# Last norm of a two-layer decoder trunk: tile 0 finished on ScalarE and GpSimd, tile 1 on VectorE, one Newton step for both

## The reference, cut to what matters

```
def layer_norm(x, g, b):
    xf = x.astype(jnp.float32)
    mu = xf.mean(-1, keepdims=True)
    var = jnp.square(xf - mu).mean(-1, keepdims=True)
    y = (xf - mu) * lax.rsqrt(var + LN_EPS) * g.astype(jnp.float32) + b.astype(jnp.float32)
    return y.astype(x.dtype)

# per layer l: mixer, first norm, then
y = hier_moe(u, w_grp[l], b_grp[l], w_router[l], b_router[l], w_gate[l], w_up[l], w_down[l])
x = layer_norm(ALPHA * x + (1 + gt2) * y, ln2_g[l], ln2_b[l])
```

## Time and profile before

| what | value |
|---|---|
| median of three runs | 802.78 us |
| the profiled execution, its own time | 802.34 us |
| span of its trace | 800.6 us |
| VectorE busy over the span | 394.2 us (49%) |
| ScalarE busy | 99.2 us (12%) |
| GpSimd busy | 72.7 us (9%) |
| mean DMA rate over the span | 365 GB/s |

### The profile page before, as it was taken

One profiled execution on the slowest core, in us unless ns is written; L12 is line 12 of the kernel. 1 busy time (PEld: TensorE's weight loads), 2 busy tenths in 40 slices (PEclk: granted clock), 3 DMA queues, 4 the chain that ended last, 5 costly groups with the idle time before them and its releaser, 6 DMA issues.

```text
span 800.6 us, 9178 instructions
## 1 busy us (share of the span) xinstructions
PE 775.4 (97%) x3776; PEld 417.9 (52%) x3796; DVE 394.2 (49%) x820; ACT 99.2 (12%) x213; POOL 72.7 (9%) x94
## 2 busy tenths in 40 slices
PE   7999999999999999999999999999999999999994
PEld 3775688564434434443358568855534443443431
DVE  1048999885332341333258469728542333234135
ACT  2111201022101101110120120101201110110110
POOL 4000241401000000000004113030010000000000
PEclk9999999999999999999999999999999999999998
DMA  9996999999999999999995597976999999999971
GB/s 320 394 408 236 393 371 360 409 415 408 415 415 409 415 416 409 415 412 411 413 409 216 210 357 279 372 286 237 360 387 416 409 414 415 409 415 414 411 300 54
DMA packets 71845, 292.54 MB, mean 365 GB/s; under 512 B 4544, under 2 KB 4824, under 8 KB 63608
## 3 DMA queue, kind: packets, MB, share of 16 engines
q1 hardware_dynamic: 69312, 291.52, 91.9%
q0 software_dynamic: 1216, 0.25, 0.2%
q10 hardware_dynamic: 1272, 0.14, 0.1%
HBM read 290.84 MB, written 1.05 MB: 365 GB/s over the span
## 4 chain that ended last, share of the span: by engine, by line
PE 89%; DVE 4%; issue 3%; ACT 1%; DVEq 0%; ACTq 0%
PE bank L814 26%; PE bank L708 14%; PE bank L838 14%; PE bank L801 8%; PE bank L725 7%; PE bank L977 5%; PE bank L860 4%; PE bank L739 3%; PE bank L822 1%; PE bank L868 1%; PE bank L581 1%; DVE X L1379 1%; DVE tmp L1378 1%; PE bank L595 0%; PE bank L775 0%
## 5 line engine op out<-in xcount | busy, mean ns | idle before, releaser
L708 PE MATMUL bank<-stage,ring 128*128 128x256 f32 x512 | 113.6, 381 | 0.2 <-ACT stage L1078 0.2
L708 PEld LDWEIGHTS bank<-stage,ring 128*128 128x128 f32 x512 | 96.2, 190 | 17.5 <-issue 4.3
L1268 DVE SCALAR_TENSOR_TENSOR bench<-ring,cond,bench 128x1024 f32<-128x1024 f32 x63 | 86.8, 1380 | 2.9 <-DMA ring<-in_w_ada_dram 0.8
L838 PE MATMUL bank<-ring,hb 128*64 128x512 f32 x384 | 85.0, 595 | 1.4 <-ACT hb L1117 1.4
L814 PE MATMUL bank<-ring,qT 128*64 128x512 f32 x384 | 84.7, 594 | 0.0
L814 PE MATMUL bank<-ring,gate_row 128*64 128x512 f32 x384 | 84.4, 594 | 0.0
L1491 DVE SCALAR_TENSOR_TENSOR kT<-bank,share,v_flat 128x512 f32<-128x512 f32 x32 | 23.9, 748 | 92.3 <-PE bank L838 92.3
L801 PEld LDWEIGHTS bank<-ccT,X 128*128 128x128 f32 x512 | 61.5, 197 | 10.8 <-issue 10.8
L801 PE MATMUL bank<-ccT,X 128*128 128x128 f32 x512 | 64.3, 284 | 0.1
L1478 DVE TENSOR_TENSOR o_sig<-o_sig,bank 128x512 f32<-128x512 f32 x16 | 11.0, 687 | 98.9 <-issue 80.4
L725 PE MATMUL bank<-ring,stage 128*128 128x512 f32 x128 | 56.0, 594 | 0.0
(11 more groups left out here) (292 smaller groups left out, 772.1 us busy)
## 6 DMA issues: line engine op xcount, KB each, us to landing
ring<-in_w_gate_dram SPq DMA_DIRECT2D x24, 2048.0 KB, 17.0
ring<-in_w_up_dram SPq DMA_DIRECT2D x24, 2048.0 KB, 19.4
ring<-in_w_down_dram SPq DMA_DIRECT2D x24, 2048.0 KB, 17.6
ring<-in_w_ada_dram SPq DMA_DIRECT2D x23, 2048.0 KB, 14.2
ring<-in_w_in_dram SPq DMA_DIRECT2D x13, 2048.0 KB, 17.0
ring<-in_w_out_dram SPq DMA_DIRECT2D x4, 2048.0 KB, 13.1
bench<-in_w_gate_dram SPq DMA_DIRECT2D x4, 2048.0 KB, 15.2
stage<-in_w_gate_dram SPq DMA_DIRECT2D x4, 2048.0 KB, 18.4
```

Of the source, the lines that this page charges most:

```text
L708: last = pe.matmul(bank[4 + i // 2][:, i % 2 * SEQ:(i % 2 + 1) * SEQ], w[:, j, col:col + P], uT[:, 4 * k + j, :], start=(k == 0 and j == 0 ...
L838: last = pe.matmul(bank[6 + half][CAP * j:CAP * (j + 1), :], hhT[:, f, CAP * j:CAP * (j + 1)], ring[s[h]][:, 4 * j + 2 * i + half, :], sta ...
L1268: ins = dve.scalar_tensor_tensor(out=sums, in0=w[:, j, :], scalar=cond[:, kc, 0:1], in1=sums, op0=ALU.mult, op1=ALU.add)
```

## The change

On VectorE, layer 1's order becomes: centre 0, one Newton step for both columns of rstd (n = 2: four tiny instructions), centre 1, finish 1. The Newton step's last instruction signals `nmr_ready` instead of holding VectorE. finish 0 leaves VectorE. ScalarE scales tile 0 by rstd in place, 1024 columns, and signals `hat_act`. GpSimd, behind its `iota`, waits for that and adds `ln_b` to tile 0 in place, 1024 columns, and signals `y_ready`, which SP's first store now waits for. The two stores of tile 1 stay behind it in SP's list; the value that the last waits for is one less, because tile 0 no longer counts on `x_ready`.

```diff
-            sp.wait_ge(x_ready, 2 * T * (DEPTH - 1) + T + 1)
+            sp.wait_ge(y_ready, 2 * DEPTH + 1)
             sp.dma_start(out[0, 0:P, :], X[:, 0, :]).then_inc(stored, 16)
             for cols, done in in_halves:
-                sp.wait_ge(done, DEPTH + 1 if done is half_ready else 2 * T * DEPTH)
+                sp.wait_ge(done, DEPTH + 1 if done is half_ready else 2 * T * DEPTH - 1)
                 sp.dma_start(out[0, P:SEQ, cols], X[:, 1, cols]).then_inc(stored, 16)
...
             pool.iota(parked[:, :], pattern=[[1, G]], base=0, channel_multiplier=0, allow_small_or_imprecise_dtypes=True)
+            pool.wait_ge(rows_spread, 6 * DEPTH - 1)
+            pool.wait_ge(hat_act, T * (DEPTH - 1) + 1)
+            pool.tensor_tensor(X[:, 0, :], X[:, 0, :], ln_b[:, :], ALU.add).then_inc(y_ready, 1)
...
+                if l + 1 == DEPTH:
+                    act.wait_ge(nmr_ready, (T + 1) * l + 2)
+                    act.activation(X[:, 0, :], X[:, 0, :], ACT.Copy, scale=rstd[:, 0:1]).then_inc(hat_act, 1)
...
-                link(dve.tensor_tensor(rstd[:, first:first + n], rstd[:, first:first + n], nt[:, first:first + n], ALU.mult))
+                last = dve.tensor_tensor(rstd[:, first:first + n], rstd[:, first:first + n], nt[:, first:first + n], ALU.mult)
+                if done is None:
+                    link(last)
+                else:
+                    last.then_inc(done, 1)
...
                 def finish(t):
-                    for cols, done in ([(slice(0, D), x_ready)], in_halves)[t]:
+                    for cols, done in in_halves:
...
                 link(centre(0))
-                newton(0, 1, rs_ready, T * (2 * l + 1) + 1)
-                finish(0)
+                newton(0, T, rs_ready, T * (2 * l + 1) + T, nmr_ready)
                 link(centre(1))
-                newton(1, 1, rs_ready, T * (2 * l + 1) + 2)
                 finish(1)
```

More of the change, by code:

```diff
@@ L1240, in modulate_half, with newton @@
                                       mod[:, 1, kc:kc + 1], mod[:, 0, kc:kc + 1], ALU.mult, ALU.add).then_inc(uT_dve, 1)
-            def newton(first, n, ready, value):
+            def newton(first, n, ready, value, done=None):
                 dve.wait_ge(ready, value)
```

## The result

The changed kernel takes 805.21 us (median of 20 runs, 803.54 to 805.74), the kernel before 804.25 us on the same count (802.64 to 804.57). The ratio is 1.0013 with a 95% interval of 1.0007 to 1.0019: about 1.05 us slower. That is under the 0.2% that I called no change, and of the sign forecast, but 805.21 lies outside the range of 802.0 to 804.9.

The account below looks back on a forecast made before the run. TensorE, busy 97% of the span, bounds the kernel; only what follows the last matmul can move. Add's end 796.34 + 4.81 gives span 801.15 against 800.6, +0.55; median 802.78 + 0.55 = 803.33 us, range 802.0 to 804.9.

Parts of the forecast that it names:

- the likeliest case: End of layer 1's norm: GpSimd's add starts before finish 1, which waits; span +0.55 us, chance 0.46.
- span ends behind that: Output stores: from the end of GpSimd's add to the end of the span, 4.81 us.
- tail: Time from the start of the first centring instruction to the end of the span; 9.81 us before the change.
- The bounds of 1.04 and 6.9: GpSimd's add of 1024 columns: 1.04 us at one-input select pace, 6.9 from the all-reduce; 2.15 taken.
- The 403: Final stores: 1049 KB flow back to back at 403 GB/s for 2.60 us.
- The break-even point of 1.60 us: GpSimd's add: the change breaks even if the add takes 1.60 us, ending at 795.79.
- Rivals 1 and 2: VectorE's finish 1 first; add waits one half (+1.45, chance 0.20) or both (+2.15; chance 0.17 including a long add).
- Rival 3: GpSimd's add takes only 1.04 us, ends at 795.23; span 800.05, -0.55 us; chance 0.15.
- Rival 4: GpSimd's add needs code not loaded, stopping it behind the wait; some +11 us; chance 0.02.
- the slow rival: Rival 2: both halves of finish 1 keep GpSimd's add out; +2.15 us; chance 0.17 including a long add.
- The third sign of being wrong: Work ahead of the norm's end: the prediction is wrong if anything before 790 us moves.

Follow-up runs that it names:

- VectorE first: Changed kernel with GpSimd's add also waiting for the first half of finish 1; from first centring to span end 12.30 us, ratio to before 1.0023.
- with one input: Changed kernel with finish 1 reading the PSUM bank in place of X, so only one SBUF input; first centring to span end 10.96 us, ratio to before 1.0016.

## Why the prediction was right and wrong

The mechanism held in each of its steps, and the likeliest case is the one that came. In us after the first centring, forecast and measured:

| step | forecast | measured |
|---|---|---|
| Newton step ends | 2.16 | 2.19 |
| ScalarE's scaling ends | 3.35 | 3.37 |
| GpSimd's add starts | 3.40 | 3.52 |
| the add's length | 2.15 | 2.34 |
| the add ends | 5.55 | 5.86 |
| span ends behind that | 4.81 | 5.07 |
| tail | 10.36 | 10.93 |

Three terms of the sum were too small, and they make the difference between +0.55 and +1.12.

- "By a signal that takes some 0.04" was carried over to GpSimd as 0.05. ScalarE's end at 796.14 to the add's start at 796.29 is 0.15, and 0.18 with VectorE first.
- The add: 2.34 where I took 2.15 from the broadcast and a second read. The bounds of 1.04 and 6.9 held. The estimate of 2.25, worked out from the page "GPSIMD Engine Reference" of the Trainium skill, section "Performance versus the Vector engine", was nearer. With 512 columns it took 1.26 to 1.27.
- Behind the add: the 1049 KB took 2.7 us from 799.48 to 802.2 (386 GB/s, not 403), and 1.5 us followed, not 1.38. The 403 was tile 0's store alone; the prediction's own times for both tiles, 1.30 and 1.43 (797.79 to 799.22), already add up to 2.73.

The break-even point of 1.60 us for the add is lower with these terms: the changed tail equals 9.81 with an add of 9.81 - 3.52 - 5.07 = 1.22 us.

Contention: "If the add is first (794.19 against 794.31), finish 1 waits until about 796.34" was right, and the first half of finish 1 has the 2.8 forecast (2.86). But the margin was 0.02 us instead of 0.12 (796.29 against 796.31), because GpSimd's signal was mis-sized by as much, so that the order came out as forecast was partly luck. It held at 0.02 to 0.03 in all five profiles in which nothing forced another. Also right was "The wait costs nothing beyond the add": with one input the wait goes and the tail stays, in SP's order as it is. In VectorE's own terms the hold undid the gain: finish 1 ends 7.06 us after the first centring, against 6.76 before and 4.96 without the add.

Rivals 1 and 2 describe the other order; VectorE first, forced, gave 12.30. With the exclusive hold for whole instructions that the page "SBUF — State Buffer" of the Trainium skill states, in its section "Who interferes with whom", all five profiles agree in which a VectorE instruction with two SBUF inputs met the add. Rival 3, the short add of 1.04, would with the measured terms have given a tail of 9.63, 0.18 less than before; that the stores in a row are its floor is what the run without the add bears out. VectorE's end at 795.75 doesn't bind there as the prediction says: with 3.05 behind it that is 798.80, 1.25 before the 800.05. Two sums of the rivals are 0.03 and 0.04 off: 797.21 + 4.81 is 802.02, and 797.90 + 4.81 is 802.71. Neither changes a verdict. Rival 4 didn't occur: the add directly behind the iota started without a stop.

What put the time outside the range is another step: "so the forecast for the median is 802.78 + 0.55 = 803.33". It takes the median of three runs as the level of the kernel before. Two of the three lay in the lower group and one, 804.18, in the upper, which is chance; over 20 runs the median is 804.25, 1.47 higher. Of the 1.88 us between 803.33 and 805.21, 1.47 are that level and 0.41 the sizes above. The range held the change (+0.96 between the medians) and not the level, though 804.18 stood in the numbers shown: an upper end of 804.18 and the slow rival's 2.15, about 806.3, would have held it.

The third sign of being wrong, "if anything before 790 us moves", did come: in the profile the norm begins 1.98 us later. The changed kernel profiled again begins it only 0.50 later (791.29), so 1.48 are not the edit's; the 0.50 stay open. The dip of TensorE's granted clock near 18 us explains the groups as far as profiles reach; it couldn't be seen in the trace of before, which has none.

## What to carry to other kernels

Work moved to another engine is worth what its result gates: here the engine relieved would have gained 1.8 us undisturbed, and the first output store went out 2.5 us later and dragged the rest with it, so look at who sends the first bytes and what then queues behind them. Give GpSimd a piece short enough to end under an instruction of VectorE that reads PSUM, and expect each of the two to shut the other out for a whole instruction as soon as VectorE reads two SBUF tensors. And where the runs shown fall into two groups, carry both through the range before adding a small difference to their median.

## What the runs showed of the hardware beyond that

A wait in the chain can be real, long (2.1 us) and free as long as something else holds what stands behind it; only taking its cause away showed it. GpSimd takes up a signal in 0.15 to 0.18 us where ScalarE and SP need 0.02 to 0.04. SP's store issues, 0.33 to 0.47 us long, follow one another 0.4 to 0.8 us apart even when their data are ready (with one input 798.53, 798.95 and 799.73).
